# Triangle parts of a chunked recurrence as 128-row diagonal blocks: one matmul for two heads

## The reference, cut to what matters

```
def step(S, inp):
    w_t, k_t, v_t, kk_t, a_t = inp[:5]
    sa = jnp.einsum('bhvk,bhk->bhv', S, kk_t)
    S = (S * w_t[:, :, None, :] - sa[..., None] * (kk_t * a_t)[:, :, None, :]
         + v_t[..., None] * k_t[:, :, None, :])
    return S, (jnp.einsum('bhvk,bhk->bhv', S, inp[5]) if emit else None)
```

## Time and profile before

| | us |
|---|---|
| timed runs, median of 3 | 4880.79 (4872.91 to 4885.07) |
| profiled execution, its own time | 4860.47 |
| span of that execution | 4858.8 |
| TensorE matmul busy | 4220.1 (87%) |
| VectorE busy | 2264.5 (47%) |
| ScalarE busy | 1472.0 (30%) |
| GpSimd busy | 603.6 (12%) |
| granted TensorE clock, mean | 0.927 |

### The profile page before, as it was taken

How to read it: one execution, slowest core, us unless ns; L and a number is a source line. 1 busy time by engine, 2 the same in 40 slices (tenths; PEclk the granted TensorE clock), 3 DMA queues, 4 the chain that set the end, 5 groups by cost and what they waited for, 6 DMA issues and landing times. The chain is left out here.

```text
span 4858.8 us, 85667 instructions
## 1 busy us (share of the span) xinstructions
PE 4220.1 (87%) x35896; PEld 3618.4 (74%) x35896; DVE 2264.5 (47%) x3566; ACT 1472.0 (30%) x2492; POOL 603.6 (12%) x769
## 2 busy tenths in 40 slices
PE   6687799999988769987999885799999995859999
PEld 5554588888864458886998764688888884558998
DVE  4454443334635544444443425543336753854444
ACT  2254321212224322123222333421223333632222
POOL 2011100001101232221000101100001112520000
PEclk8898999999989679998999887799999997869999
DMA  4446322222346852203332325422222344633332
GB/s 165 144 138 198 126 61 68 60 60 65 120 142 211 282 152 56 49 25 125 97 98 75 100 79 155 148 68 62 63 62 64 107 133 136 185 127 104 96 91 83
DMA packets 682259, 532.12 MB, mean 110 GB/s; under 512 B 128701, under 2 KB 605153, under 8 KB 681920
## 3 DMA queue, kind: packets, MB, share of 16 engines
q1 hardware_dynamic: 657024, 453.21, 31.0%
q0 software_dynamic: 24896, 73.98, 4.3%
HBM read 442.98 MB, written 84.11 MB: 108 GB/s over the span
## 5 line engine op out<-in xcount | busy, mean ns | idle before, releaser
L87 PE MATMUL acc<-h_hi,w_hi 128*128 128x258 f32 (+2 forms) x4416 | 1401.6, 317 | 44.7 <-DVE w_lo L460 32.4
L89 PE MATMUL acc<-h_hi,w_lo 128*128 128x258 f32 (+2 forms) x4416 | 1398.0, 317 | 0.0
L88 PE MATMUL acc<-h_lo,w_hi 128*128 128x258 f32 (+2 forms) x4416 | 1396.6, 316 | 0.0
L87 PEld LDWEIGHTS acc<-h_hi,w_hi 128*128 128x128 f32 x4416 | 832.5, 189 | 111.2 <-DVE w_lo L460 33.8
L88 PEld LDWEIGHTS acc<-h_lo,w_hi 128*128 128x128 f32 x4416 | 833.3, 189 | 60.6 <-issue 0.5
L89 PEld LDWEIGHTS acc<-h_hi,w_lo 128*128 128x128 f32 x4416 | 832.9, 189 | 59.0
L460 DVE TENSOR_TENSOR w_lo<-staged,w_hi 128x1024 fp32r<-128x1024 f32 (+1 forms) x414 | 488.6, 1219 | 134.9 <-ACT w_hi L338 132.0
L338 ACT CAST w_hi<-staged 128x1024 fp32r<-128x1024 f32 (+1 forms) x414 | 407.3, 1028 | 457.0 <-PE acc L89 364.0
L501 DVE COPY offset<-acc 128x2 f32<-128x2 f32 x276 | 43.8, 159 | 926.4 <-PE acc L89 923.5
L87 PE MATMUL acc<-hidden_hi,w_hi 128*128 128x512 f32 (+1 forms) x1200 | 419.3, 349 | 44.9 <-DVE hidden_lo L593 44.9
L88 PE MATMUL acc<-hidden_lo,w_hi 128*128 128x512 f32 (+1 forms) x1200 | 418.9, 349 | 0.0
(11 more groups left out here) (473 smaller groups left out, 6225.1 us busy)
## 6 DMA issues: line engine op xcount, KB each, us to landing
staged<-in_w_ffn_in SPq DMA_DIRECT2D x88, 512.0 KB, 4.4
staged<-in_ffn_w_in SPq DMA_DIRECT2D x88, 512.0 KB, 4.4
wmod<-in_w_mod SPq DMA_DIRECT2D x8, 3072.0 KB, 10.6
wmod<-in_mod_w SPq DMA_DIRECT2D x8, 3072.0 KB, 13.0
wmod<-in_mod_w SPq DMA_DIRECT2D x16, 1536.0 KB, 10.1
staged<-in_ssd_w_in SPq DMA_DIRECT2D x42, 512.0 KB, 4.2
rows<-acum SPq DMA_DIRECT2D x40, 512.0 KB, 5.3
wmod<-in_w_mod SPq DMA_DIRECT2D x8, 2048.0 KB, 7.8
```

Source lines behind the costliest of these rows:

```text
L87: nc.tensor.matmul(out, w[0], x[0], start=start, stop=False)
L88: nc.tensor.matmul(out, w[0], x[1], start=False, stop=False)
L89: return nc.tensor.matmul(out, w[1], x[0], start=False, stop=stop)
```

## The change

The level tiles become one tile `levels_of` of [128, slot, direction, level, 4, 2, 64], so that a level of a pair of heads is 128 rows by 128 columns. The even head's part stands in the upper left 64x64 and the odd head's in the lower right; the other two quarters are zero, from a memset of the whole tile by GpSimd at the start of the stage. GpSimd writes each level in two operations, one for each half of the partitions. TensorE's `each` gives way for this product alone to `level`: one matmul per pair of heads with the 128x128 block as weights and `x` [128, 64] as the moving operand, 4 instead of 8.

```diff
-        lev = [[[sb(f"lev{s}{d}{n}", [P, H, CH]) for n in range(LEV)] for d in range(2)] for s in range(2)]
+        levels_of = sb("levels", [P, 2, 2, LEV, H, 2, CH])
+        lev = [[[levels_of[:, s, d, n] for n in range(LEV)] for d in range(2)] for s in range(2)]
...
-                 "y_c", "stored0", "stored1", "passed"]
+                 "padded", "y_c", "stored0", "stored1", "passed"]
...
+                def level(out, lhs, rhs, name):
+
+                    apart()
+                    for h in range(H):
+                        mm = nc.tensor.matmul(out[:, h], lhs[:, h].rearrange("p a c -> p (a c)"), rhs[:, h], start=True, stop=True)
+                    mm.then_inc(S[name], 1)
...
-                            each(one[d], lev[s][d][n], x[s][d], "lx_p")
+                            level(one[d], lev[s][d][n], x[s][d], "lx_p")
...
-                            op = nc.gpsimd.tensor_tensor(lev[s][d][n][:], lt[s][d][:], wide(masks[:, d, 4 + n, :]), ALU.mult)
+                            for g, c in enumerate(corners):
+                                m = masks[c, d, 4 + n, :].rearrange("p (o c) -> p o c", o=1).to_broadcast([HD, H, CH])
+                                op = nc.gpsimd.tensor_tensor(lev[s][d][n][c, :, g, :], lt[s][d][c], m, ALU.mult)
...
+                nc.gpsimd.memset(levels_of[:], 0.0).then_inc(S["padded"], 1)
                 pool.wait_ge(S["masks_loaded"], 16)
+                pool.wait_ge(S["padded"], 1)
                 levels(0, 0)
```

## The result

The changed kernel took 4922.5 us (median of 4, 4914.7 to 4928.4) against 4880.4 for the kernel before. The ratio is 1.0087, 95% interval 1.0067 to 1.0106, so 42 us more (33 to 52), where +55 and a range of 4905 to 4962 us had been forecast. The profiled execution has a span of 4926.7 us.

A forecast was written before the change was run, and what follows sets the result against it. TensorE's queue was taken to bound the changed stage. Products and shape switches 53.3, the first chunk's wait 5.6 and slow clock 2, less 6 of gaps, gave +55 us on 4880.8: 4936 us, range 4905 to 4962.

The forecast's parts named there:

- The product: TensorE's level product: 8 whole-array passes of 0.111 us, 0.89 us against 0.47, so 0.42 us dearer.
- The changes of shape: TensorE switching between 64*64 and whole-array passes around a pair of level products: 0.17 us more going in, 0.15 coming out.
- chunk 0's wait: TensorE waits in the first chunk for GpSimd's building of direction 1's levels: 5.6 us lost, ends 0 and 6.
- my 53.3: Sum in us on TensorE over the stage for dearer level products and switches of shape, after swallowed waits for `z`.
- GpSimd: Building the levels: twenty operations a chunk at 0.76 us each, 15.2 us, costing nothing except in the first chunk.
- The clock: TensorE's granted clock drops after its idle time in the first chunk: 2 us added.
- The gaps: TensorE's idle time called issue, without a releaser: 6 of 33 us taken back, ends 0 and 33.
- a sign of being wrong: The prediction is wrong if TensorE's issue gaps shrink by more than 20 us.
- The instruction rival: TensorE's gaps come from instructions arriving too slowly, so nearly all 33 us go: +28 us, 4909 us; 12%.
- The rival of a cheap whole-array pass: In TensorE's level products a whole-array pass runs at 29 ns: -25 us, 4856 us; 3%.
- the rival of GpSimd as the bound of a chunk: GpSimd's level operations take 1.5 us each, so eleven chunks wait 3.2 us: +35 us, 4971 us; 3%.
- that of nearly nothing: In the stage, all gaps gone, no cost switching out, half-price GpSimd operations: +11 us, 4892 us; 3%.

The follow-up runs named there:

- e6_half_columns: Changed kernel with each whole-array level matmul cut into two of all 128 rows and 64 weight columns; 4891.1 us, ratio 1.0039.
- e1_pool_only: Changed kernel with the old product of 8 64*64 matmuls on the new tiles, keeping the memset and GpSimd's twenty operations; 4878.4 us, ratio 1.0010.
- e3_between: Changed kernel with the next chunk's part for direction 0 moved between the two directions' level products in levels 1 to 4; 4908.8 us, ratio 1.0070.
- e5_wide_twice: Changed kernel with each whole-array level product issued twice, same result; 4997.3 us, ratio 1.0243.
- the second pair of profiles: The kernel before and the changed kernel each run and profiled once more without edit; 4870.7 and 4920.4 us.
- c0_before: The kernel before run and profiled once more, no edit; 4870.7 us, ratio 0.9993.
- e7_narrow_twice: The kernel before with each 64*64 level product issued twice, same result; 4910.5 us, ratio 1.0089.

## Why the prediction was right

**The product.** Right in mechanism and size. I took 0.111 us a pass from another stage, and it is 0.111 here, also when doubled. e6_half_columns shows the reason more exactly than I gave it: it is not that half of the array's rows are zeros, but that 128 columns of weights go into one matmul. I had named both the doubled columns and the loss of a neighbour to run beside; which of them it is stays open.

**The changes of shape.** Each step was as forecast: the loads show 0.203 and 0.259 us, which is 0.17 and 0.15 over the usual. Over the stage the steps into, within and out of level products add up to 146.6 us against 89.0 before. Less chunk 0's wait that is 50.7 us more, against my 53.3. The nearness hides something. Of the 89.0 us, 8 are gaps called issue that fell inside a level product or just before one, and the changed kernel has under 1 of those. Without them the product and its changes cost 58.0 us, 4.7 more than forecast. Some 4 us of that are the three further waits at level 3 and nineteen passes at 0.213 us a step, twice the usual: six in chunk 0's first product and thirteen soon after the gap of 3.9 us between two chunks.

**GpSimd.** An operation on 64 partitions takes 0.741 us on average where one on 128 took 0.796 in the stage's group, and twenty of them take 15.92 us at the start where I had 15.2: 0.80 us each against the upper bound of 0.76 that I chose. So chunk 0's wait was 6.7 us (5.6 forecast), and e1_pool_only puts the whole GpSimd side at 5 us. The memset took 8.63 us (8.6) and was hidden.

**The clock.** In the 10 us around the wait the granted clock is 0.83, 1.7 us of full speed lost (2 forecast), and all 64\*64 steps together grew by 3 us.

**The gaps.** I took back 6 of the 33 us that stood outside the level products; there they shrank by 3.5 and by about 7 in the two pairs of profiles. With those inside or just before the level products, which I had left out, all gaps together shrank by 10.8 and 17.7 us. That is still under the 20 us that I had named as a sign of being wrong. The instruction rival (33 us back) did not happen here, though e3_between and e5_wide_twice show that half of the gaps can go when TensorE's pace changes.

Together 58.0 + 6.9 + 3.1 - 10.8 is 57 us for a stage that grew by 56.6 (52.3 in the second pair of profiles). That the sum came out so near to the 55 us forecast is partly luck: a product taken 4.7 us too cheap and gaps of which 4.8 us too few were taken back cancel. The rival of a cheap whole-array pass, the rival of GpSimd as the bound of a chunk and that of nearly nothing are all excluded by the same rows. What was off is the last step, the carrying over from a profile to the medians: the forecast of 4936 us is 13 above the measured 4922.5, since 55 us of path gave 42 and 46 us there.

## What to carry to other kernels

In float32 and with 64 moving columns, a block-diagonal matmul saved no time here, because the small ones already run side by side in different corners of the array. Before merging, compare start-to-start steps of the exact shape, which another stage of the same program may hold, rather than the durations of single matmuls, which differ by little (218 and 275 ns) where the steps differ fourfold. If only the contraction is made deeper and the output columns stay apart, the pass keeps its pace, and only changes of shape are paid. Work for the next chunk is best placed just where the queue waits for another engine.

## What the runs showed that was not expected

- A VectorE operation with all operands in SBUF was held up by GpSimd's building: `z<-z,masks` went from 0.83 to 1.37 us with GpSimd's longer operations, and ended 0.28 us after the running one each time. The Trainium skill, "GPSIMD Engine Reference", section Architecture, says that GpSimd's SBUF ports are shared with VectorE; by that VectorE would be late here, and the trace agrees with those numbers.
- TensorE's gaps without a releaser fall in fixed places: in the first profile of the kernel before, those above 0.45 us in the first chunk and a half stand ahead of passes 249, 373, 745, 869, 992, 1117 and 1241, counted in weight loads from the first level product as 0. That is 124 passes or a multiple of it apart to within one, also in the middle of a product. In c0_before the large ones stand at the same places with other lengths. The longest, 3.6 to 4.0 us in all eleven traces, stands between the eighth and the ninth chunk, where the hardware loop starts its second turn. Slow passes added (e5_wide_twice) or spread out (e3_between) brought them from 38 to 17 and 19 us; quick passes added (e7_narrow_twice) did not make them grow. What sets their length stays open, and with it how much of a saving on this queue can be kept.
